# A Mamba-2 scan that makes y transposed: x and the state stationary, the decay and C streamed

## The reference

```python
def ssd_mixer(u, w_in, conv_w, conv_b, dt_bias, a_log, d_skip, norm_w, w_out):
    zxbcdt = u @ w_in
    z, xbc, dt = jnp.split(zxbcdt, [...], axis=-1)
    xbc = jax.nn.silu(causal_dwconv(xbc, conv_w, conv_b))
    xs, b_in, c_in = jnp.split(xbc, [...], axis=-1)
    dt = softplus(dt + dt_bias);  a = -jnp.exp(a_log) * dt
    x_dt = xs * dt                                       # per head
    a_cum = jnp.cumsum(a, axis=-1)                       # within a chunk of 128
    decay = jnp.exp(segsum(a))                           # exp(a_cum[l] - a_cum[s]), l >= s
    cb = jnp.einsum('bclgn,bcsgn->bcgls', cc, bc)
    y_diag = jnp.einsum('bcgls,bgrcls,bcsgrp->bclgrp', cb, decay, x_dt)
    decay_states = jnp.exp(a_cum[..., -1:] - a_cum)
    states = jnp.einsum('bclgn,bgrcl,bclgrp->bcgrpn', bc, decay_states, x_dt)
    ...                                                  # states carried over chunks
    y_off = jnp.einsum('bclgn,bcgrpn,bgrcl->bclgrp', cc, states, jnp.exp(a_cum))
    y = y_diag + y_off + xs * d_skip
    yg = rms_norm(y * jax.nn.silu(z), norm_w)            # per group of 256 channels
    return yg @ w_out
```

## Time and profile before

| | us |
|---|---|
| median of 3 runs | 1626.69 (1624.33 to 1631.54) |
| profiled execution | 1628.21, its span 1626.1 |
| busy: PE | 1555.3 (96% of the span) |
| busy: DVE | 1271.5 (78%) |
| busy: ACT | 715.2 (44%) |
| busy: POOL | 621.7 (38%) |
| moved by DMA | 292.75 MB |

### The profile page before, as it was taken

One profiled execution on the slowest core, in us unless ns is written; L12 is line 12 of the kernel. 1 busy time (PEld: TensorE's weight loads), 2 busy tenths in 40 slices (PEclk: granted clock), 3 DMA queues, 4 the chain that ended last, 5 costly groups with the idle time before them and its releaser, 6 DMA issues. The chain is left out here.

```text
span 1626.1 us, 26163 instructions
## 1 busy us (share of the span) xinstructions
PE 1555.3 (96%) x7468; PEld 1255.0 (77%) x7468; DVE 1271.5 (78%) x2319; ACT 715.2 (44%) x1229; POOL 621.7 (38%) x747
## 2 busy tenths in 40 slices
PE   6999999999999999999999986999999999999996
PEld 5778888878888788888888875777777777777774
DVE  6668868768778778688687787998788878788884
ACT  5333232223332233332222443765666665666662
POOL 2222131131131231311311312376676767666664
PEclk9999999999999999999999997999999999999998
DMA  4121121221121221221212565999999999999992
GB/s 159 40 82 53 50 81 33 59 73 37 50 72 46 60 72 31 68 58 46 84 33 72 177 229 186 375 367 368 376 370 372 373 372 375 372 379 366 369 347 69
DMA packets 142996, 292.75 MB, mean 180 GB/s; under 512 B 21597, under 2 KB 72205, under 8 KB 142897
## 3 DMA queue, kind: packets, MB, share of 16 engines
q1 hardware_dynamic: 127904, 266.29, 46.8%
q0 software_dynamic: 14992, 25.22, 4.3%
HBM read 291.81 MB, written 25.30 MB: 195 GB/s over the span
## 5 line engine op out<-in xcount | busy, mean ns | idle before, releaser
L2056 DVE TENSOR_TENSOR gu_lo<-w_gu,gu_hi 128x1024 fp32r<-128x1024 f32 x256 | 306.4, 1223 | 50.0 <-ACT gu_hi L1895 37.4
L1318 PE MATMUL proj<-uTh,wl 128*128 128x512 f32 x768 | 308.8, 402 | 6.7 <-issue 4.1
L1320 PE MATMUL proj<-uTh,wh 128*128 128x512 f32 x768 | 301.2, 392 | 0.0
L1319 PE MATMUL proj<-uTl,wh 128*128 128x512 f32 x768 | 300.3, 391 | 0.0
L1895 ACT ACTIVATE gu_hi<-w_gu 128x1024 fp32r<-128x1024 f32 x256 | 261.0, 1054 | 59.7 <-PE g_ps L1968 35.5
L557 POOL TENSOR_TENSOR wl<-raw,wh 128x512 fp32r<-128x512 f32 x96 | 129.3, 1364 | 384.6 <-ACT wh L645 384.6
L1318 PEld LDWEIGHTS proj<-uTh,wl 128*128 128x128 f32 x768 | 144.9, 189 | 37.3 <-issue 7.2
L1320 PEld LDWEIGHTS proj<-uTh,wh 128*128 128x128 f32 x768 | 144.8, 189 | 31.8
L698 ACT ACTIVATE xbc<-v 128x512 f32<-128x512 f32 x64 | 40.5, 633 | 292.0 <-DVE v L1035 292.0
L1319 PEld LDWEIGHTS proj<-uTl,wh 128*128 128x128 f32 x768 | 145.2, 189 | 28.7
L1035 DVE SCALAR_TENSOR_TENSOR v<-xr,cw,v 128x512 f32<-128x512 f32 x192 | 146.1, 761 | 14.7 <-DVE v L1031 0.5
(11 more groups left out here) (310 smaller groups left out, 3285.2 us busy)
## 6 DMA issues: line engine op xcount, KB each, us to landing
w_gu<-in_moe_w_gate_dram SPq DMA_DIRECT2D x128, 512.0 KB
w_gu<-in_moe_w_up_dram SPq DMA_DIRECT2D x128, 512.0 KB
w_d<-in_moe_w_down_dram SPq DMA_DIRECT2D x128, 512.0 KB
raw<-in_ssd_w_in_dram SPq DMA_DIRECT2D x96, 256.0 KB, 3.5
E<-acum_dram SPq DMA_DIRECT2D x64, 256.0 KB, 3.4
raw<-in_ssd_w_out_dram SPq DMA_DIRECT2D x28, 256.0 KB, 2.8
hacc<-in_x_dram SPq DMA_DIRECT2D x8, 512.0 KB, 7.5
out_dram<-hacc SPq DMA_DIRECT2D x8, 512.0 KB, 5.1
```

What stands on the lines that cost most here:

```text
L1318: nc.tensor.matmul(out, al, bh, start=start, stop=False)
L1319: nc.tensor.matmul(out, ah, bl, start=False, stop=False)
L1320: return nc.tensor.matmul(out, ah, bh, start=False, stop=stop)
L2056: vec.tensor_tensor(wl[:, j % RING, :], weights.gate_up(b, j), wh[:, j % RING, :].bitcast(F32), ALU.subtract).then_inc(w_lo, 1)
```

## The change

`scan` now puts out y with channels on partitions. For C times the state, `S` is stationary (two halves of 128 channels) and C is streamed. For the chunk's own part `xdt` of a head is stationary (128 x 64) and `E` is streamed (128 columns); heads 0 and 2 go to partitions 0 to 63 of `y_ps`, heads 1 and 3 to 64 to 127. `turn_y` is gone, and so is `ysb` as a copy of y with tokens on partitions. exp of the decay sums is needed along the free axis now, so ACT takes it once of the transposed sums (`ace`), SP stores it to `eac_dram`, and `load_ee` fetches, per chunk, two rows for each half of the partitions into `EE` (one buffer, two transfers). On DVE `y_from_state` multiplies half 0 by `EE` into `ysb`, `y_in_chunk` adds D times x to half 1 into `ygf`, and `gate` adds the two and multiplies by silu(z). Counts of semaphores (`sums`, `gates`, `Y_STEPS`, `G_STEPS`) follow.

```diff
@@ SP
+            def load_ee(G, c):
+                if c == NT:
+                    return
+                wait(sp, y_steps, G, Y_STEPS, sums(c - 1) + 1 if c > 1 else 0)
+                rows_c = eac_dram[bass.ds(val(G, NT * R, c * R), R), :].rearrange("(t q) l -> q t l", q=2)
+                for q in range(2):
+                    half_p = slice(q * HEAD_DIM, (q + 1) * HEAD_DIM)
+                    sp.dma_start(EE[half_p], rows_c[q].partition_broadcast(HEAD_DIM)).then_inc(ee_loaded, 16)
...
                     if not last:
                         for what, place in early[c] + late[c]:
                             load_piece(G, what, place)
+                    if c < NT - 1 or not last:
+                        load_ee(G, c + 1)
@@ ACT, once
-                nc.scalar.activation(eac[:].rearrange(flat), y_ps[:, 0, :], ACT.Exp).then_inc(cum_act, 1)
...
+                    nc.scalar.activation(ace[:, j, :], st_ps[:, 0, j * P:(j + 1) * P], ACT.Exp).then_inc(acT_sb, 1)
@@ DVE
+            def y_from_state(G, c):
+                wait(dve, y_mm, G, NT, c + 1)
+                if c % NT:
+                    wait(dve, gate_steps, G, G_STEPS, gates(c))
+                    wait(dve, ee_loaded, G, 32 * (NT - 1), 32 * c)
+                    vec.tensor_tensor(ysb[:], y_ps[:, 0, :], EE[:].rearrange("p t l -> p (t l)"), ALU.mult).then_inc(y_steps, 1)
+
+            def y_in_chunk(G, c):
+                H, cc = (G, c) if c < 8 else (nxt(G), c - 8)
+                wait(dve, ylo_done, G, 2 * NT, 2 * c)
+                for t in range(2):
+                    vec.scalar_tensor_tensor(ygf[:, t, :], xbc[:, H[1] % 2, t, cc * P:cc * P + P], dsk[:, bass.ds(val(H, 2, t), 1)],
+                                             y_ps[:, 1, t * P:(t + 1) * P], ALU.mult, ALU.add).then_inc(y_steps, 1)
...
-                    vec.tensor_tensor(heads(ysb[:]), heads(y_ps[:, 0, :]), spread(eac, G, c), ALU.mult).then_inc(y_steps, 1)
-                    wait(dve, y_steps, G, 2 * NT - 1, sums(c) + 1)
-                    vec.tensor_tensor(ysb[:], ysb[:], y_ps[:, 1, :], ALU.add).then_inc(y_steps, 1)
...
             def gate(G, k):
-                wait(dve, yT_done, G, NT, k + 1)
-                for t in range(2):
-                    vec.scalar_tensor_tensor(ygf[:, t, :], xbc[:, par, t, cols], dsk[:, bass.ds(val(G, 2, t), 1)],
-                                             st_ps[:, 1, t * P:(t + 1) * P], ALU.mult, ALU.add).then_inc(gate_steps, 1)
+                wait(dve, y_steps, G, Y_STEPS, sums(k + 1))
+                if k:
+                    vec.tensor_tensor(ygf[:], ygf[:], ysb[:].rearrange("p (t l) -> p t l", t=2), ALU.add).then_inc(gate_steps, 1)
@@ PE
             def scan(G, c):
-                wait(pe, y_steps, G, 2 * NT - 1, sums(c))
+                wait(pe, y_steps, G, Y_STEPS, sums(c))
+                wait(pe, s_steps, G, 2 * NT - 3, updates(c))
                 if cc:
-                    wait(pe, s_steps, G, 2 * NT - 3, updates(c))
-                    nc.tensor.matmul(y_ps[:, 0, :], xbc[:, H[1] % 2, 3, cc * P:cc * P + P], S[:, c % 2, :], start=True, stop=True)
+                    for t in range(2):
+                        cols = slice(t * P, (t + 1) * P)
+                        nc.tensor.matmul(y_ps[:, 0, cols], S[:, c % 2, cols], xbc[:, H[1] % 2, 3, cc * P:cc * P + P],
+                                         start=True, stop=True)
                 wait(pe, m_done, G, NT, c + 1)
                 for r in range(R):
-                    q = slice(r * HEAD_DIM, (r + 1) * HEAD_DIM)
-                    mm = nc.tensor.matmul(y_ps[:, 1, q], E[:, c % 2, r, :], xdt[:, c % 2, q], start=True, stop=True)
+                    half_p = slice(r % 2 * HEAD_DIM, (r % 2 + 1) * HEAD_DIM)
+                    mm = nc.tensor.matmul(y_ps[half_p, 1, r // 2 * P:(r // 2 + 1) * P],
+                                          xdt[:, c % 2, r * HEAD_DIM:(r + 1) * HEAD_DIM], E[:, c % 2, r, :], start=True, stop=True)
...
-                wait(pe, gate_steps, G, 24, 3 * c)
...
-            def turn_y(G, c):
-                wait(pe, y_steps, G, 2 * NT - 1, sums(c + 1))
-                wait(pe, s_steps, G, 2 * NT - 3, updates(c + 1))
-                for t in range(2):
-                    mm = nc.tensor.transpose(st_ps[:, 1, t * P:(t + 1) * P], ysb[:, t * P:(t + 1) * P], ident[:])
-                mm.then_inc(yT_done, 1)
```

More of the change, by code:

```diff
@@ L137, in __init__, with mamba @@
         self.h_stored = [sem(f"h_stored{b}") for b in range(2)]
-def mamba(nc, hacc, rt, weights, xg, spare, x, norm_w, w_in, conv_w, conv_b, dt_bias, a_log, d_skip, y_norm, w_out, acum_dram,
+def mamba(nc, hacc, rt, weights, xg, spare, x, norm_w, w_in, conv_w, conv_b, dt_bias, a_log, d_skip, y_norm, w_out, acum_dram, eac_dram,
           norm2_w, w_group, w_expert, b_group, b_expert, u2_dram, out):
@@ L150, in mamba @@
     LASTG = GROUPS - 1
+    Y_STEPS = 3 * NT - 1
+    G_STEPS = 2 * NT - 1
     with ExitStack() as ctx:
@@ L207, in mamba @@
         tmp = [zs[:, j // 4, 256 * (j % 4):256 * (j % 4) + 256] for j in range(8)]
-        acs, rows, dall = sq, ygf, ysb[:, 0:NH]
+        acs, rows, dall, ace = sq, ygf, ysb[:, 0:NH], ygf
         u2, wb2 = xbc[:, 0, 0:2, :], xbc[:, 0, 3, :]
@@ L277, in mamba @@
         cbm_done = sem("cbm_done")
+        ee_loaded = sem("ee_loaded")
         e_loaded = [sem(f"e_loaded{j}") for j in range(2)]
@@ L474, in _ @@
             for j in range(2):
-                sp.wait_ge(acT_sb, j + 1)
+                sp.wait_ge(acT_sb, 2 * j + 2)
                 sp.dma_start(acum_dram[j * P:(j + 1) * P, :], acs[:, j, :]).then_inc(acT_stored, 16)
-            sp.wait_ge(acT_stored, 32)
+                sp.dma_start(eac_dram[j * P:(j + 1) * P, :], ace[:, j, :]).then_inc(acT_stored, 16)
+            sp.wait_ge(acT_stored, 64)
             load_e(G0, 0)
             load_e(G0, 1)
+            load_ee(G0, 1)
             for half in range(2):
@@ L496, in body @@
                             load_piece(G, what, place)
+                    if c < NT - 1 or not last:
+                        load_ee(G, c + 1)
                     if last and c == 1:
-                        wait(sp, gate_steps, G, 24, 1)
+                        wait(sp, gate_steps, G, G_STEPS, 1)
                         wait(sp, conv_steps, G, 32, 32)
@@ L701, in tanh_unit @@
                     if half == 0:
-                        wait(act, gate_steps, G, 24, -12)
+                        wait(act, gate_steps, G, G_STEPS, gates(NT // 2) - G_STEPS)
                     nc.scalar.activation(zs[:, t - 4, cols], proj_ps[i % 2][:], ACT.Tanh, scale=0.5
@@ L718, in gated @@
             def gated(G, k):
-                wait(act, gate_steps, G, 24, 3 * k + 3)
+                wait(act, gate_steps, G, G_STEPS, gates(k + 1))
                 nc.scalar.activation(sq[:], ygf[:], ACT.Square).then_inc(sq_done, 1)
@@ L1088, in make_m, with state @@
                 vec.tensor_tensor(E[:, c % 2], E[:, c % 2], cb, ALU.mult).then_inc(m_done, 1)
-            def y_and_state(G, c):
[L1091 to L1095, removed]
-                    vec.tensor_tensor(heads(ysb[:]), heads(y_ps[:, 0, :]), spread(eac, G, c), ALU.mult).then_inc(y_steps, 1)
-                    wait(dve, y_steps, G, 2 * NT - 1, sums(c) + 1)
-                    vec.tensor_tensor(ysb[:], ysb[:], y_ps[:, 1, :], ALU.add).then_inc(y_steps, 1)
+            def y_from_state(G, c):
[10 more added lines that the diff above has]
+                                             y_ps[:, 1, t * P:(t + 1) * P], ALU.mult, ALU.add).then_inc(y_steps, 1)
+            def y_and_state(G, c):
+                y_from_state(G, c)
+                y_in_chunk(G, c)
+                state(G, c)
+            def state(G, c):
                 if c == NT - 1:
@@ L1200, in last_chunks @@
                 gate(G, NT - 2)
-                y_and_state(G, NT - 1)
+                y_from_state(G, NT - 1)
                 gated_low(G, NT - 2)
+                y_in_chunk(G, NT - 1)
                 mean_square(G, NT - 2)
-                wait(dve, ylo_done, G, 2 * NT, 2 * (NT - 1))
                 gate(G, NT - 1)
@@ L1553, in ranks_first @@
                 pe.wait_ge(table_consts, 10)
-                wait(pe, gate_steps, (None, LASTG), 24, 3 * NT)
+                wait(pe, s_steps, (None, LASTG), 2 * NT - 3, updates(NT))
                 nc.tensor.matmul(ranks[:, 0:SPLIT * NE], tri16, A[:, 0:SPLIT, :].rearrange("p i e -> p (i e)"),
```

24 lines of the change are left out of this document (11 added, 13 removed).

## The result

The changed kernel takes 1631.84 us (median of 20 runs) against 1625.88 for the kernel before (20 runs). The ratio is 1.004, 95% interval 1.0028 to 1.0051: slower by 0.4 per cent, where 1614.6 was forecast. Its profiled execution took 1631.54 us, span 1629.6.

What follows compares the result with a forecast made beforehand. TensorE was taken to bound the steady groups. -12.9 - 3.4 + 2.2 + 2.0 = -12.1 us turned the profiled 1628.2 into 1616.1, and 1.5 less for the median gave 1614.6 us; 8-in-10 range 1590 to 1632.

Steps and rivals of the forecast that it cites:

- PE's steady terms: TensorE in the scan's steady groups: -12.9 us for transposes, -3.4 for C times state, +2.2 for the four products.
- transposes: Steady groups: 56 pairs of transposes of y leave TensorE at 0.23 us each, -12.9 us.
- The split of C times state: One 256-column product becomes two of 128 columns, 0.44 instead of 0.52 us; 0.07 taken for 49 chunks, -3.4 us.
- The four products: x stationary, decay streamed: eight records take 0.88 us instead of 0.84 in 56 chunks, +2.2 us.
- Rival B: Four products: the halves run beside each other, -22 us instead of +2.2, about 1590 us; chance 0.17.
- the one row of the same stream: Profile row of a 128-column fp32 product, 0.11 us a record, used to price the four products at 0.88 us.
- The gate: TensorE's 6.0 us wait for the squares, where VectorE reaches the gate late: left unchanged, bounds -3 and +3.
- The row fetch: SP's queue in a middle group: E issued some 2.5 us later but hidden with 1.5 us to spare, cost 0.
- The last group: Last scan group: E lands 1 to 3.5 us late, 0 to 13 us over five chunks; +2 us taken in sum.
- rival D: Queue in the last group eats the gain: E late by 2.6 us on five chunks, 13 us, about 1626; chance 0.15.
- What would show it: Signs in the changed profile: steady groups shrink from 800 to 786 us, TensorE over 98 per cent busy.
- the chance of slower: Whole kernel: 0.13 for slower, beside 0.70 for faster and 0.17 for the same, within 0.5 per cent or 8.1 us.

Runs made afterwards that it cites:

- one half: Changed kernel with all four products of x and decay writing partitions 0 to 63: 1642.21 us, ratio 1.0076 to the kernel before.
- full width: Changed kernel with 128 stationary columns in the four products, which write all 128 partitions: 1634.92 us, ratio 1.0033 to the kernel before.
- the order on SP: Changed kernel with the decay rows of chunk c fetched right behind the fetch of E(c+1): 1614.88 us, ratio 0.9909 to the kernel before.
- the sum out of the gate: On top of the order on SP, the sum of y's two parts moved right behind the state's update: 1603.73 us, ratio 0.9828 to the kernel before.

## Why the prediction was wrong, point by point

- *PE's steady terms*: transposes -0.23, right, nothing stands between the products that follow. The split of C times state was -0.07 and is +0.10 (0.01 of it the split, 0.09 the change of width). The four products were +0.04 and are -0.26, and the state's product +0.05. The sum, -0.34 a chunk, is a little better than -0.26. Rival B was therefore half right: the halves run beside each other, but their gain of 0.43 pays 0.31 for the half width. The Trainium skill, TensorEngine Tiling (Array Packing), Tiling Modes, spoke on both sides. The pairing is shown by one half against both (1.01 and 0.58); a drain fits the 0.09 and 0.10 that full width saves. I let the one row of the same stream decide instead of taking both rules together: -0.43 and +0.31 on 0.89 give 0.77, 0.07 under the 0.84 of before.
- *The gate, taken at 0 with bounds -3 and +3*: wrong. I read 178 us of idle VectorE as cover. Around chunk 3 it has none: from the state's update to the gate its operations follow one another for 7 us. From one chunk's products to the next squares PE now needs 0.5 us less (10.07 against 10.55) and the squares come 0.3 later (11.40 against 11.11). PE's idle time in the steady groups grew by 10.9 us, 8.6 of them before the squares (some by E itself, for which VectorE now waits 5.2 us in 4 chunks). That turns 56 x -0.34 = -19 into -8; 7.1 is seen. The wait for the squares, now 14.6 us, lost 4.1 with the order on SP and 6.3 more with the sum out of the gate, so the hold had a part in it too. The one SBUF operation beside GpSimd had taken 1.49 in the kernel before, where 587 was only the mean of the earlier trace rows; now there were two of them. I had priced the sum by that mean and so as a cost in VectorE's work, not as a wait at the one place where PE follows it.
- *The row fetch, "hidden, with 1.5 us to spare"*: read at one middle chunk. E lands in 3.8 us there (before 3.4), not 5.7, yet VectorE waits for it at four group starts, where it wants E sooner than in the chunk of the earlier trace rows. The hold cost the steady groups about 4 us, taken at 0.
- *The last group, +2*: the step that failed. The mechanism was described as rival D (pieces held back, then in front of E), with 2.6 us a chunk as its ceiling, from an 0.88 us reserve; the wait was 16.8 us over five, 3.4 each. I reckoned E behind 2.7 MB from 940 on, but not that ScalarE's and PE's lateness delays the next multiplication and so the next burst (argued from the order of the waits, no run takes it apart). I looked past `last_wo`: a load issued once, at the boundary, behind the same wait. It cost about 4 us. And I put the clock at nothing: PE's added idle time is 7.5 us, and 17.7 us at 1.2 GHz cost about 8.9 more, though the earlier trace rows already showed 0.92 for this stage. 14.0 stands where 2 stood; this alone takes the forecast of -12 to 0, and the rest is the steady groups'.
- *What would show it*: the window of the steady groups was to shrink to 786 with PE over 98 per cent busy; PE is 97.3 per cent busy. E's landing grew in the last group (5.7 to 8.8) and hardly elsewhere (3.4 to 3.8), and ScalarE waited there, as named.
- *The range*, 1590 to 1632, held the time by 0.2 us; the chance of slower, 0.13, was too small for a change that puts a wait ahead of every transfer on the queue.

## What to carry to other kernels

A DMA that needs a wait belongs at the place in the queue's program where that wait is already over. List everything that stands behind it, the loads issued once at a boundary too: here two lines in another order are worth 1.3 per cent. An average idle time is no cover either: read the few chunks in which the bound engine waits at all, and what the engine it waits for does in the 8 us before. Last, read the granted clock by stage as well, since TensorE's waits can be paid for twice, as idle time and as a lower clock behind it: in the last group the second was worth 8.9 us, more than the 7.5 of the first.

## What was not expected of the hardware

- Column halves run beside each other with fp32 operands of 64 stationary columns: eight records in 0.58 us, 1.01 when all go to one half. Going to half width costs 0.09 us on PE's path, coming back 0.10, and the half-width records 0.12 more than as many of full width where they don't pair.
- Two transfers of 64 KB to 64 partitions hold SP's queue for 1.2 to 1.4 us a pair (median 0.61 each), one of 256 KB to all 128 for 0.35.
- VectorE's 0.42 us operation on two SBUF operands takes 0.88 to 1.5 beside GpSimd's subtraction of 128x512 (two in 2.71 us).
- TensorE's clock fell to 1.2 GHz behind single idle gaps of 1.2 to 2.3 us, though not behind all of them, and stood there for 17.7 of the 80.4 us of the changed kernel's last scan.
